# Retention's value products from fp32 matmuls to three fp32r products of high parts and remainders

## The reference

```python
def retention_mixer(x, w_in, norm_g, w_out):
    q, k, v, g = split_cols(x @ w_in, RET_SPLITS)      # 4 heads, q and k 256 wide, v 512 wide
    q, k = rotary(q), rotary(k) * RET_DK ** -0.5
    o = head_group_norm(retention_chunked(q, k, v), norm_g)
    return (o * silu(g)) @ w_out
...
        s = einsum('bihd,bjhd->bhij', qc, kc) * decay_intra
        o = einsum('bhij,bjhv->bihv', s, vc) + einsum('bihd,bhdv->bihv', qc, state) * decay_q
```

## Time and profile before

| | |
|---|---|
| median of 3 runs | 1630.9 us (1630.23 to 1631.37) |
| time of the profiled execution | 1629.91 us |
| its span, first to last instruction | 1628.1 us |
| granted TensorE clock | 0.999 of full |
| PE busy | 1616.3 us, 99% |
| DVE busy / ACT busy | 951.5 us / 773.4 us |

### The profile page before, as it was taken

The page is one execution under the profiler, slowest core; times in us unless marked ns, Lnnn a source line. Parts: engine busy times, 40 slices in busy tenths (PEclk is TensorE's granted clock), DMA queues, the critical chain, the costliest instruction groups (busy, mean ns, idle before and its releaser), DMA issues.

```text
span 1628.1 us, 18405 instructions
## 1 busy us (share of the span) xinstructions
PE 1616.3 (99%) x7782; PEld 1342.5 (82%) x7782; DVE 951.5 (58%) x942; ACT 773.4 (48%) x810; POOL 77.9 (5%) x99
## 2 busy tenths in 40 slices
PE   9999999999999999999999999999999999999998
PEld 6888897788888888888988888888888997888886
DVE  6555466676544685455658545665445557585553
ACT  7444446655443774442655434354443435454340
POOL 0121000000000000001010000000000141000000
PEclk9999999999999999999999999999999999999999
DMA  9756474466554765463647645665465654575460
GB/s 314 214 179 219 163 239 130 155 209 211 182 179 158 254 224 181 155 213 105 233 156 242 193 158 207 203 195 188 164 206 181 197 179 142 181 233 191 160 217 26
DMA packets 221921, 306.74 MB, mean 188 GB/s; under 512 B 8768, under 2 KB 144064, under 8 KB 221712
## 3 DMA queue, kind: packets, MB, share of 16 engines
q1 hardware_dynamic: 216944, 290.02, 54.2%
q0 software_dynamic: 4320, 14.95, 2.9%
q10 hardware_dynamic: 576, 0.59, 0.1%
HBM read 304.49 MB, written 1.05 MB: 188 GB/s over the span
## 4 chain that ended last, share of the span: by engine, by line
PE 97%; DVE 2%; ACT 1%; issue 0%; DMA 0%; ACTq 0%; DVEq 0%
PE bank L644 28%; PE bank L655 28%; PE bank L648 25%; PE bank L608 3%; PE bank L659 3%; PE bank L686 2%; PE bank L689 2%; PE bank L688 2%; DVE low L1497 0%; ACT hiw L1132 0%; DMA g0T<-in_g0T 0%; PE bank L1018 0%; PE bank L826 0%; PE bank L807 0%; PE bank L786 0%
## 5 line engine op out<-in xcount | busy, mean ns | idle before, releaser
L1497 DVE TENSOR_TENSOR low<-raw,hiw 128x2048 fp32r<-128x2048 f32 (+2 forms) x296 | 633.1, 2148 | 389.4 <-ACT hiw L1132 389.3
L1132 ACT ACTIVATE hiw<-raw 128x2048 fp32r<-128x2048 f32 (+1 forms) x281 | 522.2, 1865 | 358.3 <-DMA raw<-in_ffn_w_out 85.8
L644 PE MATMUL bank<-hiw,xh 128*128 128x512 f32 x1404 | 385.0, 396 | 0.2 <-ACT xh L1137 0.2
L655 PE MATMUL bank<-low,xh 128*128 128x512 f32 x1404 | 376.0, 390 | 0.0
L648 PE MATMUL bank<-hiw,xl 128*128 128x512 f32 x1232 | 330.1, 390 | 0.0
L655 PEld LDWEIGHTS bank<-low,xh 128*128 128x128 f32 x1404 | 263.5, 188 | 55.7 <-DVE low L1497 0.2
L644 PEld LDWEIGHTS bank<-hiw,xh 128*128 128x128 f32 x1404 | 257.0, 188 | 53.0 <-issue 2.5
L648 PEld LDWEIGHTS bank<-hiw,xl 128*128 128x128 f32 x1232 | 231.3, 188 | 49.6
L644 PE MATMUL bank<-hiw,th 128*128 128x512 f32 x528 | 144.8, 392 | 0.0
L648 PE MATMUL bank<-hiw,tl 128*128 128x512 f32 x528 | 143.3, 389 | 0.0
L655 PE MATMUL bank<-low,th 128*128 128x512 f32 x528 | 143.2, 389 | 0.0
(11 more groups left out here) (250 smaller groups left out, 1157.3 us busy)
## 6 DMA issues: line engine op xcount, KB each, us to landing
raw<-in_ffn_w_in SPq DMA_DIRECT2D x176, 512.0 KB, 4.8
raw<-in_ffn_w_out SPq DMA_DIRECT2D x40, 1024.0 KB, 4.9
raw<-in_ret_w_in SPq DMA_DIRECT2D x24, 1024.0 KB, 5.1
raw<-in_ffn_w_gate SPq DMA_DIRECT2D x43, 512.0 KB, 4.2
raw<-in_ffn_w_up SPq DMA_DIRECT2D x43, 512.0 KB, 5.4
raw<-in_ffn_w_down SPq DMA_DIRECT2D x20, 1024.0 KB, 4.9
raw<-in_w_in SPq DMA_DIRECT2D x16, 1024.0 KB, 5.5
raw<-in_gla_w_in SPq DMA_DIRECT2D x12, 1024.0 KB, 5.0
```

The costliest lines, as they stand in the source:

```text
L644: pe.matmul(o[:, :], tokens(0, k), whi[:, k, :], start=start and k == 0, stop=False, skip_group_check=True)
L655: ins = pe.matmul(o[:, :], tokens(0, k), wlo[:, k, :], start=False, stop=end, skip_group_check=True)
L1132: act.activation(hiw[s][:, 0:n], raw[s][:, 0:n], ACT.Copy).then_inc(hi.mark(i), 1)
L1497: dve.tensor_tensor(low[s][:, c0:c1], raw[s][:, c0:c1], hiw[s][:, c0:c1].bitcast(F32), ALU.subtract).then_inc(lo.mark(*what), 1)
```

## The change

The three fp32 matmuls of a head's values become nine of type fp32r. The values have a high part `rvh` (ACT's copy, as `rv` before, other type) and a remainder `rvl`, a new subtraction of DVE from the PSUM bank. `rvl0` (t = 0) lies over `xn`, which is not in use here, `rvl1` in the second half of slot 6. The decayed scores are now called `rsp` and lie in the rest of slot 5; ACT copies them to the high part `rsh`, and DVE writes the remainder `rsl` in place over `rsp`. Where PE waited for ACT's `rv` before it used a bank again, it now waits for DVE's `rvl`.

```diff
@@ build @@
-                rv = sb("rv", [P, 2, 2048], F32, in1)
+                rvh = sb("rvh", [P, 2, 2048], F32R, in1)
...
-            rsT = sb("rsT", [P, 4, 384], F32, ar)
+            rsh = sb("rsh", [P, 4, 384], F32R, ar)
...
             rtmp = sb("rtmp", [P, 2, 2, 512], F32, ar)
             rgn = sb("rgn", [P, 512], F32, ar)
+            with ExitStack() as in1:
+                rsp = sb("rsp", [P, 4, 384], F32, in1)
+            rsl = sb("rsl", [P, 4, 384], F32R, ar)
...
             rg0 = sb("rg0", [P, 2048], F32, ar)
+            rvl1 = sb("rvl1", [P, 2048], F32R, ar)
...
+        with ExitStack() as ar:
+            rvl0 = sb("rvl0", [P, 2048], F32R, ar)
         xn = sb("xn", [P, 2, D])
@@ pe_ret @@
-                            pe.wait_ge(fn.sem, fn.of("rv", n - 2, t))
+                            pe.wait_ge(vec.sem, vec.of("rvl", n - 2, t))
...
-                        pe.wait_ge(fn.sem, fn.of("rv", 2 + hf, 1))
+                        pe.wait_ge(vec.sem, vec.of("rvl", 2 + hf, 1))
@@ values(hd) @@
-                pe.wait_ge(vec.sem, vec.of("rs", hd))
+                pe.wait_ge(vec.sem, vec.of("rsl", hd))
                 if hd == 0:
-                    pe.wait_ge(fn.sem, fn.of("rv", 3, 1))
+                    pe.wait_ge(vec.sem, vec.of("rvl", 3, 1))
...
-                    if t:
-                        pe.matmul(b[:, :], rsT[:, hd, P:2 * P], rv[:, 0, c], start=True, stop=False,
-                                  skip_group_check=True)
-                        ins = pe.matmul(b[:, :], rsT[:, hd, 256:384], rv[:, 1, c], start=False, stop=True,
-                                        skip_group_check=True)
-                    else:
-                        ins = pe.matmul(b[:, :], rsT[:, hd, 0:P], rv[:, 0, c], start=True, stop=True,
+                    for s in range(t + 1):
+                        q = slice(t * P, t * P + P) if s == 0 else slice(256, 384)
+                        pe.matmul(b[:, :], rsh[:, hd, q], rvh[:, s, c], start=s == 0, stop=False, skip_group_check=True)
+                        pe.matmul(b[:, :], rsh[:, hd, q], rvl[s][:, c], start=False, stop=False, skip_group_check=True)
+                        ins = pe.matmul(b[:, :], rsl[:, hd, q], rvh[:, s, c], start=False, stop=s == t,
                                         skip_group_check=True)
@@ act_ret @@
+            def scores_high(hd):
+                act.wait_ge(vec.sem, vec.of("rs", hd))
+                act.activation(rsh[:, hd, :], rsp[:, hd, :], ACT.Copy).then_inc(fn.mark("rsh", hd), 1)
+
+            scores_high(0)
             for n in range(4):
                 act_high(act, ahead(at["rg"][2 * n + 1]))
...
                 if n < 3:
+                    scores_high(n + 1)
                     norms(n)
@@ dve_ret @@
-            dve_lead(dve, "ret", at["rv"][0:4])
-            dve_lows(dve, ahead(at["rv"][7]))
+            def unit(n, t):
+                c = slice(n * 512, n * 512 + 512)
+                dve.wait_ge(fn.sem, fn.of("rv", n, t))
+                dve.tensor_tensor(rvl[t][:, c], PAIRS[n % 2][t][:, :], rvh[:, t, c].bitcast(F32), ALU.subtract).then_inc(
+                    vec.mark("rvl", n, t), 1)
+
+            dve_lead(dve, "ret", at["rv"][0:4], unit)
+            for n in (2, 3):
+                dve_lows(dve, ahead(at["rv"][2 * n + 1]))
+                unit(n, 0)
+                unit(n, 1)
...
+            def scores_low(hd):
+                dve.wait_ge(fn.sem, fn.of("rsh", hd))
+                dve.tensor_tensor(rsl[:, hd, :], rsp[:, hd, :], rsh[:, hd, :].bitcast(F32), ALU.subtract).then_inc(
+                    vec.mark("rsl", hd), 1)
...
             for n in range(4):
                 dve_lows(dve, ahead(at["rg"][2 * n + 1]))
+                if n == 0:
+                    scores_low(0)
                 if n < 3:
                     scores(n + 1)
                     norms(n)
+                    scores_low(n + 1)
```

More of the change, by code:

```diff
@@ L266, in build @@
         gsT, gsX = xn[:, :, 0:512], xn[:, 1, 512:1024]
+        rvl = (rvl0, rvl1)
         tiles, at = [], {}
@@ L1417, in unit @@
                 act.wait_ge(passed.sem, passed.of(at["rv"][2 * n + 1], t))
-                act.activation(half(rv[:, t, 1024 * (n // 2):], n % 2), PAIRS[n % 2][t][:, :], ACT.Copy).then_inc(
+                act.activation(half(rvh[:, t, 1024 * (n // 2):], n % 2), PAIRS[n % 2][t][:, :], ACT.Copy).then_inc(
                     fn.mark("rv", n, t), 1)
@@ L1898, in scores @@
                 for a, z in ((0, 256), (256, 384)):
-                    dve.tensor_tensor(rsT[:, hd, a:z], b[:, a:z], dec[:, hd, 0:z - a], ALU.mult).then_inc(
+                    dve.tensor_tensor(rsp[:, hd, a:z], b[:, a:z], dec[:, hd, 0:z - a], ALU.mult).then_inc(
                         vec.mark("rs", hd), 1)
+            def scores_low(hd):
+                dve.wait_ge(fn.sem, fn.of("rsh", hd))
+                dve.tensor_tensor(rsl[:, hd, :], rsp[:, hd, :], rsh[:, hd, :].bitcast(F32), ALU.subtract).then_inc(
+                    vec.mark("rsl", hd), 1)
             def norms(hd):
```

## The result

The changed kernel takes 1629.11 us (median of 20 runs, 1628.81 to 1629.74); the kernel before took 1631.18 beside it (20 runs, 1630.23 to 1631.80). The ratio is 0.9987, its 95% interval 0.9981 to 0.9993. The difference of the medians is 2.07 us, and the interval leaves out 1. The profiled execution took 1629.25 us.

A forecast was written before the change was run, and what follows sets the result against it. The retention stage was taken as bound by PE's queue of matmuls. 2.1 us saved on products less 0.1 us of stall at the turn-round gave -2.0 us, from 1630.9 to 1628.9 us, range 1627.8 to 1630.6.

The forecast's parts named there:

- The matmuls: Each head's values on PE: nine matmuls take 2.05 us in place of 2.57, saving 2.1 us for four heads.
- the two outer rivals: Values on PE: nine matmuls don't overlap, 1634.7 us, chance 0.03; or distance falls to weight load, 1627.4 us, chance 0.03.
- The values' stage: DVE's eight `rvl` subtractions, 0.68 us each, lie in its idle time; cost 0.
- The scores' parts: `rsh` on ACT takes 0.5 us, `rsl` on DVE 0.56; head 0's `rsl` leaves 1.1 us before PE's weights.
- The table load: On ACT, the square root's table load runs right behind the `rsh` copy, moving the norm 0.98 us later.
- The turn-round: Head 1's transposes after values(3) need head 0's `rol`: 0.1 us margin left, 0.1 us stall taken, ends 0 and 0.5.
- The sum: Whole kernel: -2.1 + 0.1 = -2.0 us, giving 1628.9 us from 1630.9.
- The span: Span of the profiled execution after the change: 1626.1 us.
- The rival that I gave 0.12: ACT's or DVE's chain 1 us longer at `turn_out(1, 1)` or values(0): stall of 1 to 1.5 us, 1630.2; chance 0.12.

The follow-up runs named there:

- experiment 1: Changed kernel with all new ACT and DVE parts made and waited for, but three fp32 products a head on PE from the high parts; 1631.13 us.
- experiment 4: Changed kernel, complete, plus a square root of a constant on ACT ahead of the scores' copy, loading the table earlier; 1629.25 us.
- Experiment 10: Changed kernel with six more DVE subtractions ahead of head 0's `rsl`, and POOL's gate multiplication waiting until they are done; 1631.09 us.
- experiment 3: Changed kernel with only the high parts' product on PE, plus a square root of a constant ahead of the scores' copy on ACT; 1623.52 us.
- experiment 6: Changed kernel with three more DVE subtractions ahead of head 3's `rsl`, results unused; 1630.33 us.
- experiment 9: Changed kernel with six more DVE subtractions ahead of head 0's `rsl`, results unused, POOL not moved; 1634.54 us.

## Why the prediction was right

**The matmuls.** Forecast 2.05 us a head from the distance of 0.2275 us in the pass ahead; measured 2.04, in all four heads (values(0), for one, from 1341.33 to the scores at 1343.37). 4 x (2.57 - 2.04) = 2.1, and 2.08 were found between the two fixed points. Experiments 1 and 4 show that nothing else takes part. The same distance ends the two outer rivals: the nine didn't fall apart into records of 0.39 us, and the distance didn't fall to the weight load of 188 ns, let alone to the 131 ns that the Trainium skill (TensorE: Matmul & The Clock Gate, "Back-to-back issue gap") states for N = 512; no row here agrees with that figure.

**The values' stage.** Forecast: eight subtractions of 0.68 us in idle time, 0. Measured 0.687, cost 0 (experiment 1).

**The scores' parts.** Forecast 0.5 for `rsh` and 0.56 for `rsl`; measured 0.525 and 0.551. `rsl` of head 0 was to be 1.1 us ahead of PE's first weights. It ended at 1339.12 + 0.55 = 1339.67, and these weights load some 0.2 us ahead of 1341.33: 1.4 us. Experiment 10 confirms it in effect: 3.5 us of extra work less a wait of 1.67 leaves 1.8 us of cover, counted to the matmul itself (1341.33 - 1339.67 = 1.66).

**The table load.** Forecast: right behind the copy, and the norm 0.98 us later. It stands there, and taking it away again moved `rol` by 1.02 (experiments 3 and 4). By the drain that the Trainium skill adds to a switch (ScalarE: Activation LUTs, "What ACT_TABLE_LOAD costs"), the changed kernel would have stalled by an estimated microsecond (1.38 less the margin of 0.31); it didn't.

**The turn-round.** I put the margin at 0.1 us and took 0.1 us of stall. The place was right, and the size was off by little: the margin is 0.31 us by three experiments, and the stall 0. Most of the 0.2 us is `rol` itself: it started 0.66 us ahead of values(3) before (1385.28 - 1384.62) and 0.71 behind them now (1385.85 - 1385.14), so it moved by 1.37 instead of 1.5 us. The last 0.1 us I can't place. The stall of 0.1 us in the sum is the one term that was wrong; it was too small to matter.

**The sum.** Forecast 1628.9, measured 1629.11 beside a kernel before that ran 0.3 us higher in its longer series (1631.18 instead of 1630.9). The difference was forecast as 2.0 and came as 2.07. That 0.2% would be about what can't be told from no change was too careful: 0.13% came out with an interval that leaves out 1. The span was forecast as 1626.1 and came as 1627.5. There the step that failed was to let a single execution stand for the sum: the 1.4 us are there before the queries' stage begins, 1.0 of them the wait for data at the kernel's start. What the sum of the stage needed, the medians gave.

**The rival that I gave 0.12** was priced by one rule, a stall costs its length. That holds within 0.3 us for the 1 to 1.5 us that it spoke of (experiments 6 and 10), but would have been wrong for one of over 2 us, where the time went above the kernel before. Its suspicion of POOL was sound: the last section shows that contention in the kernel before.

## What to carry to other kernels

Where PE is busy without a gap, cost a replaced product by the distance of starts of the same shape and type in the trace, and check the result between two fixed points inside the stage, not by the span of one execution. Then list what the engines off the path moved, and look for the first place where PE picks up something of theirs: here a margin of 0.31 us decided whether a further saving of 5.5 us came in full or as 4.4, and a microsecond of ACT's table load, worthless in the changed kernel, was worth 1.0 us there. When a delay on VectorE is forecast, see whether GpSimd works at the same time. And when PE is to wait, read the granted clock behind the wait: here the waits up to 1.67 us left it full, and the traced ones from 2.17 us did not.

## What the runs showed of the hardware

**VectorE and GpSimd held each other up.** A subtraction of two tiles in SBUF took 1.54 instead of 0.55 us, and one of 128 x 2048 was 1.08 us longer than usual, when a multiplication of GpSimd was under way; GpSimd's two took 5.20 instead of 2.54. In experiment 6 GpSimd's two took 4.17 and DVE's two kept 4.48: there GpSimd alone lost. With GpSimd moved away, both went back. It fits with the Trainium skill (SBUF — State Buffer, "SBUF: two separate sides"), which says that such a VectorE operation and one of GpSimd hold a common pair of ports by turns, each for its whole instruction. The 2.72 us of one weight tile in the kernel before, which I had noted as POOL's use of memory, fits too. Beside it POOL's addition took 2.80 us, against 0.74 for the one before:

```profile
1331.36 2.80 POOL L583 TENSOR_TENSOR kr<-rtmp 128x256 f32<-128x256 f32 x1
```

In the changed kernel this tile comes later and meets none of these; POOL's same step took 0.74 us, and the two weight tiles 4.49. And where DVE's subtraction takes one of its two inputs from PSUM, nothing was stretched: POOL's two multiplications took 2.54 us beside `rol`'s 1.28.

**A long wait of PE is paid twice.** In the traced executions, behind waits of 2.17 us and more the granted clock showed windows between 0.50 and 0.89, products started 0.43 us apart instead of 0.227 (experiment 9), and the cost was 1.7 to 2.7 us above the wait. Behind 1.67 us and less it stayed at 1.00, and the cost was 0.3 us above the wait. At 2.2 us some executions seem to have kept the full clock.
